# The gates' stage of layer 1: weight panels of projection and modulation in turn, one panel loaded out of turn, sums one panel behind

## The reference

```python
mod_x = adaln_params(c, ada_w[l], ada_b[l])        # silu(c) @ ada_w + ada_b, six rows of 1024
hx = modulate(rms_norm(x, norm_mix_g[l]), mod_x[:, 0], mod_x[:, 1])
x_qkv, x_beta, x_a, x_z, x_u, x_v, x_gates = jnp.split(hx @ w_in[l], (...), axis=-1)
y_gdn = gdn_output(o_x, x_z, gdn_norm_g[l])        # rms_norm(o) * silu(z)
y_sgu = sgu_mixer(x_u, x_v, ...)                   # gelu(u) * (W_s @ layer_norm(gelu(v)) + b)
x = x + mod_x[:, 2][:, None, :] * merge_branches(y_gdn, y_sgu, x_gates, w_branch_a[l], w_branch_b[l], w_out[l])
hx = modulate(rms_norm(x, norm_ffn_g[l]), mod_x[:, 3], mod_x[:, 4])
```

## Time and profile before

| what | value |
|---|---|
| median of 3 runs | 1771.29 us (1769.92 to 1771.68) |
| profiled execution, its own time | 1775.53 us |
| its span in the trace | 1773.8 us |
| TensorE busy | 1546.5 us (87%) |
| VectorE busy | 812.2 us (46%) |
| mean granted clock of TensorE | 0.915 |
| gates' stage in the trace | 468.96 to 615.75 us |
| merge stage's first 64 instructions of L1536 | from 615.75 us, 31.00 us |

### The profile page before, as it was taken

The page is one execution under the profiler, slowest core; times in us unless marked ns, Lnnn a source line. Parts: engine busy times, 40 slices in busy tenths (PEclk is TensorE's granted clock), DMA queues, the critical chain, the costliest instruction groups (busy, mean ns, idle before and its releaser), DMA issues. The chain is left out here.

```text
span 1773.8 us, 19527 instructions
## 1 busy us (share of the span) xinstructions
PE 1546.5 (87%) x7573; PEld 901.5 (51%) x7573; DVE 812.2 (46%) x1512; ACT 371.3 (21%) x700; POOL 190.3 (11%) x280
## 2 busy tenths in 40 slices
PE   4999968789999698876789868999889899999977
PEld 2877756578644344442234323444444447656563
DVE  2344548444536558632111123356564315576553
ACT  3222245111111100110000011000450124642230
POOL 0000016500000000001000000000350001212340
PEclk9899989677899799787899988999999899999998
DMA  9331002230577677579999992524311222121120
GB/s 351 98 95 48 1 1 50 84 85 11 183 260 258 235 275 246 226 309 411 408 366 367 388 344 103 190 95 159 103 37 35 95 68 75 48 95 48 49 72 24
DMA packets 132299, 283.62 MB, mean 160 GB/s; under 512 B 28744, under 2 KB 39272, under 8 KB 126955
## 3 DMA queue, kind: packets, MB, share of 16 engines
q1 hardware_dynamic: 128608, 266.65, 42.1%
q0 software_dynamic: 3600, 15.73, 2.2%
HBM read 312.77 MB, written 4.19 MB: 179 GB/s over the span
## 5 line engine op out<-in xcount | busy, mean ns | idle before, releaser
L2707 PE MATMUL ps<-hT,ring 128*128 128x512 f32 x256 | 114.8, 606 | 3.1 <-PEq L2614 2.7
L1395 PE MATMUL ps<-ring,hTx 128*128 128x512 f32 x256 | 112.1, 594 | 1.9 <-PEq L176 1.8
L327 DVE SCALAR_TENSOR_TENSOR ada_acc<-ring,cact,ada_acc 128x512 f32<-128x512 f32 x154 | 104.1, 747 | 0.5
L631 PE MATMUL ps<-hTx,ring 128*128 128x256 f32 x384 | 91.6, 394 | 5.3 <-PEq L176 5.3
L2342 PE MATMUL ps<-hT,ring 128*128 128x512 f32 x208 | 90.4, 592 | 0.0
L631 PEld LDWEIGHTS ps<-hTx,ring 128*128 128x128 f32 x384 | 75.1, 198 | 19.8 <-issue 8.0
L2707 PEld LDWEIGHTS ps<-hT,ring 128*128 128x128 f32 x256 | 48.9, 194 | 62.9 <-issue 62.9
L1395 PEld LDWEIGHTS ps<-ring,hTx 128*128 128x128 f32 x256 | 48.3, 191 | 60.5 <-issue 60.5
L1928 PE MATMUL ps<-ring,hTx 128*32 128x512 f32 x384 | 53.8, 711 | 26.0 <-DMA ring<-in_expert_w 26.0
L722 DVE SCALAR_TENSOR_TENSOR conv<-xpad,taps,conv 128x512 f32<-128x512 f32 (+1 forms) x96 | 63.6, 663 | 3.4
L2342 PEld LDWEIGHTS ps<-hT,ring 128*128 128x128 f32 x208 | 39.5, 190 | 48.5 <-issue 48.3
(11 more groups left out here) (528 smaller groups left out, 2745.8 us busy)
## 6 DMA issues: line engine op xcount, KB each, us to landing
ring<-in_expert_w SPq DMA_DIRECT2D x24, 2048.0 KB, 15.4
far<-in_expert_w SPq DMA_DIRECT2D x24, 2048.0 KB, 18.2
ring<-in_w_in SPq DMA_DIRECT2D x16, 2048.0 KB, 11.6
ring<-in_ada_w SPq DMA_DIRECT2D x12, 2048.0 KB, 9.5
ring<-in_w_ada SPq DMA_DIRECT2D x12, 2048.0 KB, 9.3
ring<-in_w_in_c SPq DMA_DIRECT2D x10, 2048.0 KB, 7.9
ring<-in_expert_w POOLq DMA_DIRECT2D x32, 512.0 KB
far<-in_expert_w POOLq DMA_DIRECT2D x32, 512.0 KB
```

Source lines behind the costliest of these rows:

```text
L327: ins = dve.scalar_tensor_tensor(out=part, in0=slot[:, kt], scalar=c[:, kt:kt + 1], in1=part, op0=ALU.mult, op1=ALU.add)
L631: ins = pe.matmul(ps[:, j % BANKS, s * L:(s + 1) * L], slot[:, kt, (j % 4) * P:(j % 4 + 1) * P], (hTc, hTx)[s][:, kt], start=(kt == 0), st ...
L1395: ins = pe.matmul(ps[:, 2 + i % BANKS], hTx[:, kt, t * P:(t + 1) * P], stream.slot(n)[:, kt], start=(kt == 0), stop=(kt == KT - 1))
L2707: ins = pe.matmul(bank, slot[:, kt, j % 4 * P:(j % 4 + 1) * P], hT[:, kt], **edge)
```

## The change

The panels of the gates' stage are put strictly in turn: uvg0, rest0, uvg1, rest1, ..., uvg7, rest7. With that, `rest[0]` takes the list's place before `uvg[1]`. In the last delta step SyncE still loads u's second panel, now with a new method `issue_ahead`, which loads a panel ahead of the list; `issue` later skips it. The two lent slots change roles: `sc` and `by_unit` swap slots, and so do the two calls that free them. `total(k)` is called behind panel k + 1 rather than k + 2, and only `total(7)` is left for the end.

```diff
+        self.ahead = set()
...
             n = self.issued
-            if n >= RING and self.panels[n](self.slot(n)):
-                sp.wait_ge(self.used[n % RING], n // RING)
-            self.load(sp, n)
+            if n not in self.ahead:
+                if n >= RING and self.panels[n](self.slot(n)):
+                    sp.wait_ge(self.used[n % RING], n // RING)
+                self.load(sp, n)
             self.issued += 1
+
+    def issue_ahead(self, sp, n):
+
+        sp.wait_ge(self.used[n % RING], n // RING)
+        self.load(sp, n)
+        self.ahead.add(n)
...
-        for i in range(9):
-            if i < 8:
-                uvg.append(len(stream.panels))
-                add_cols(w_in, COL_Z + (2 + i) * PANEL)
-            if i:
-                rest.append(len(stream.panels))
-                add_cols(ada, (3 + i) * PANEL)
+        for i in range(8):
+            uvg.append(len(stream.panels))
+            add_cols(w_in, COL_Z + (2 + i) * PANEL)
+            rest.append(len(stream.panels))
+            add_cols(ada, (4 + i) * PANEL)
...
-                slot_a, slot_b = (stream.slot(z_in[0] + i).rearrange("p k n -> p (k n)") for i in (2, 1))
+                slot_a, slot_b = (stream.slot(z_in[0] + i).rearrange("p k n -> p (k n)") for i in (1, 2))
...
                                 if not more:
-                                    stream.issue(sp, uvg[1] + 1)
+                                    stream.issue_ahead(sp, uvg[1])
...
                                         if gi + 3 == GRP and not more:
-                                            for n in gdn_lent[0::2]:
+                                            for n in gdn_lent[1::2]:
                                                 stream.free(pe, n)
                                 if not more:
-                                    for n in gdn_lent[1::2]:
+                                    for n in gdn_lent[0::2]:
                                         stream.free(pe, n)
...
                                 stream.free(pe, n)
-                                if i // TT >= 2:
-                                    total(pe, i // TT - 2)
+                                if i // TT:
+                                    total(pe, i // TT - 1)
...
-                        total(pe, 6)
                         total(pe, 7)
```

## The result

The changed kernel took 1749.48 us (median of 3 runs, 1744.36 to 1751.16) against 1771.29 us: a ratio of 0.9872 with the 95% interval 0.9839 to 0.9905. Two repeats gave 0.9891 (0.9873 to 0.9909) and 0.9901 (0.9885 to 0.9917). Over all runs the changed kernel's median is 1750.19 us (15 runs, 1744.36 to 1755.75) and that of the kernel before 1770.01 us (76 runs, 1763.26 to 1775.86): 19.8 us faster.

What follows compares the result with a forecast made beforehand. TensorE was taken to set the gates' stage's pace, losing time to sums standing behind later panels. Terms -6.5, -7.7 and -1.5 summed to -15.7 us, from a median of 1771.29 to 1755.6 us; range 1752.5 to 1762.0.

Steps and rivals of the forecast that it cites:

- uvg2 late (rival 1): Before panel 2, u's third panel lands late and stalls TensorE 1 to 4.3 us; 1756.6 to 1763.5 us, chance 0.12.
- last tile's end, all terms: Gates' stage up to its last tile: one moved sum +1.1, waits and clock -0.6, -4.9, -1.8, -0.3; together -6.5 us.
- wait before `mix`, wait before `otok`, its clock: TensorE's waits before `mix` and the transposes of `otok` go, -0.6 and -4.9; slower clock behind the latter, -1.8 and -0.3.
- the end, last tile to merge stage: Behind the gates' last tile only rest6's sum, the last sum, their puts and a barrier remain: 5.2 us for 12.9, -7.7.
- first 64 instructions of the merge stage: Start of the merge stage: shorter idle times may keep TensorE's clock up, gain 0 to 2.9 us, taken as -1.5.
- rest of the merge stage: The merge stage's loads come in time: 0, at most 1 us.
- sum of the two stages: Gates' and merge stages: -6.5 - 7.7 - 1.5 = -15.7 us.
- all that follows: Stages behind the merge stage: no term in the sum; the range allowed 1.5 us for the clock.
- Slower (rival 3): Gates' stage: late loads and dot products make TensorE wait in each of six panels; 1775 us, chance 0.02.
- One of my signs of being wrong: Gates' stage: the forecast would be wrong if TensorE waited for a projection panel anywhere in the stage.
- I take half: Clock gain at the merge stage's start, between 0 and 2.9 us, put at -1.5.
- below 1.5 us for a clock that does better elsewhere: Allowance at the range's lower end for a better clock elsewhere, giving 1752.5 us.

Runs made afterwards that it cites:

- sums_only: The kernel before with only the sums moved to one panel behind, in the old panel order: 1760.85 us, ratio 0.9957.
- order_only: The changed kernel with the sums two panels behind as before, so only the panels' order is new: 1773.1 us, ratio 1.0015 to the kernel before.
- rest_first: The changed kernel with rest0 issued first in the gates' stage, behind only the 64 KB `gn_row`: 1753.59 us, ratio 0.9921 to the kernel before.
- after: The changed kernel itself, first measurement and trace, against the kernel before: 1749.48 us, ratio 0.9872.
- bias_late: The changed kernel with the four bias rows loaded behind u's third panel and awaited before the first put: 1751.87 us, ratio 0.9894 to the kernel before.
- the shifted one: The changed kernel with two spare products ahead of the transposes of k and v, far before the gates' stage: 1751.06 us, ratio 0.9895.
- before_again: The kernel before run once more with no edit, for a second trace: 1770.05 us, ratio 1.0007.
- before_fill: The kernel before with spare products on TensorE in the waits before the transposes of `otok` and around `total(7)`: 1763.07 us, ratio 0.9970.
- after_fill: The changed kernel with spare products in the pauses of the merge and routing stages: 1752.97 us, ratio 0.9909 to the kernel before.
- first_and_late: The changed kernel with rest0 issued first and the bias rows behind u's third panel: 1755.18 us, ratio 0.9921 to the kernel before.

## Why the prediction was right and wrong

By its own steps, with the trace of the changed kernel:

| step | forecast | measured |
|---|---|---|
| uvg2 late (rival 1) | 0, at most 4.3 | 1.4 to 1.5 |
| last tile's end, all terms | -6.5 | -5.5 |
| wait before `mix`, wait before `otok`, its clock | -0.6, -4.9, -2.1 | -0.6, -4.9, -2.1 |
| the end, last tile to merge stage | -7.7 | -7.8 |
| first 64 instructions of the merge stage | -1.5 (0 to -2.9) | -2.9 |
| rest of the merge stage | 0 | -0.3 |
| sum of the two stages | -15.7 | -16.5 |
| all that follows | 0, at most -1.5 in the range | -3.3 by the medians of all runs |

**What held.** The two waits had one cause, sums that stood a panel too late on TensorE, and all that hung on it went as worked out: the gate behind `mix`, the transposes without a wait, the end of 5.1 us for 12.9. `sums_only` shows that this edit by itself takes 9.3 us off the gates' stage; `order_only` shows that the new order by itself takes nothing off. I treated the two as one change and did not say which does what. Slower (rival 3) was far off for the changed kernel, but its mechanism is real: in `order_only` a dot product held up by a sum did stall projection panels, by 0.59 and 2.46 us.

**uvg2.** One of my signs of being wrong came true: TensorE waited for a projection panel, 1.4 to 1.5 us in every trace of the changed kernel. That is rival 1's wait, near the small end of its price, though its total did not come. I let the load land 5.1 to 5.6 us behind the one ahead of it, and that held: 5.26 us, and 5.24 in `rest_first`. What I had too early is the load ahead. I took the one issued at the end of panel 0 as done 23.9 us into the stage (492.9 - 468.96), when the engines fell idle in the old trace; in the changed kernel rest1, issued at the same point, was in use only at 25.5 us (493.15 - 467.67). Why it came 1.6 us later is not shown; uvg2 was in the queue beside it from 21.0 us on (488.71 - 467.67). The margin, near 0, could not take that. The edits show two limits: in a full queue uvg2 follows the load ahead (`after`, `rest_first`); with less ahead it still took 9.7 us from its issue, with the bias rows beside it (`bias_late`), and the wait went only with both edits.

**The clock at the merge stage.** "I take half" was the mis-sized term: the clock held in all four traces of the changed kernel, the shifted one included. By the rule of the Trainium skill that I quoted (TensorE: Matmul & The Clock Gate, "HAM oscillation — how this bites in real kernels") it would hold, and the trace agrees: 28.07 us with an idle time of 1.83 us. Behind the merge stage the runs do not bear out that single gaps decide: at the wait for w_out's panel the clock fell with an idle time of 2.50 us (8.60 us for 16 instructions, `before_again`) and held with one of 3.24 (7.13 us, `sums_only`). `before_fill` gives the price of the clock in these two stages directly: 5.9 us by the stages, 5.3 by the ratio.

**What made the result fall outside the range** is none of these. The two stages gave 16.5 us, within 1 us of the forecast. The step that failed is "below 1.5 us for a clock that does better elsewhere": all that follows the merge stage I had put at nothing, and allowed 1.5 us for it in the range. By the medians of all runs it was 3.3 us (19.8 - 16.5). The first result lay 5.3 us beyond the two stages; 2.0 of these are the luck of two medians of 3 runs, 1771.29 for 1770.01 and 1749.48 for 1750.19.

The single traces show even more than 3.3 us in two stages that the change does not touch, w_out and routing: on average 51.0 and 23.1 us in the three unedited or shifted traces of the kernel before, 48.2 and 21.1 in four of the changed one, 4.8 together. So they can't be added up to the medians' 3.3. The w_out rows above tell how such a difference arises: TensorE's clock was low behind the wait for w_out's panel in the one and not in the other. Why a pause of nearly the same length lowers it in one kernel and not in the other stays open. Low there were also `order_only`, `bias_late` and `rest_first` (8.83 us each); at the upper level were `before_fill`, `sums_only`, `after_fill` and `first_and_late` (7.13 us each). So both levels occur with the sums of either place and with either order of the panels. Two small edits of the changed kernel's first loads, each by itself, brought the low level, and both together the upper one. Seven traces with 3 to 4 of each kind may still be chance, and that the change itself causes these 3.3 us is not shown.

The range was also too narrow for a plainer reason: single executions of one kernel spread from 1763 to 1776 us, and a median of 3 runs can lie about 1 us from that of many.

## What to carry to other kernels

When one engine's program order holds a result back for another (here a sum that stands a panel behind its data), look for every wait that names it: two waits and the stage's end had the same cause, and moving one call per panel took 9 us off. Reordering loads gains only if whoever frees the slots is not held up by something else, so measure the two edits of such a pair apart. Where TensorE waits for some us, price the wait with the slower clock behind it; here that was a third of what the two stages won.

## What the runs showed of the hardware that I had not expected

- Spare products that fill the long waits kept the clock at its upper level and saved 5.3 us without removing a wait (`before_fill`); in smaller pauses they moved the fall to where it cost more (`after_fill`, 74.9 us for 69.2).
- In a full queue a 2 MB load came 5.2 to 5.3 us behind the one ahead of it (`after`, `rest_first`), as the rate of 376 to 408 GB/s says. Counted from its own issue it took 9.7 and 12.0 us there, and still 9.7 us where the queue had nearly run dry before it (`bias_late`, 90 GB/s). So the rate tells when a load lands only if it is known when the one ahead does.
- The same program's later stages, from the experts to the end, took 1002.4 and 1010.7 us in two traces of the kernel before, so a difference of a few us between single traces outside the changed stages says nothing.
